# A routed mixture of experts: gating inside the expert block, and a scatter that adds rows in memory

## The reference, cut to what matters

```python
def hierarchical_moe(xn, w_rg, b_rg, w_re, b_re, w_g, w_u, w_d):
    ...                                  # a group and 2 of its 8 experts for each token: expert_idx, gates
    # 32 experts, blocks of 128 rows; each expert's rows are padded to whole blocks
    x_pad = jnp.zeros((n_blocks * MOE_BLOCK, d), xt.dtype).at[dest].set(xt[token_idx[order]])
    def expert_block(args):
        xb, e = args
        hb = jax.nn.silu(xb @ w_g[e]) * (xb @ w_u[e])
        return hb @ w_d[e]
    y = y_pad[dest] * gates[order][:, None].astype(y_pad.dtype)
    out = jnp.zeros((t, d), xt.dtype).at[token_idx[order]].add(y)
x = x + hierarchical_moe(rms_norm(x, norm_ffn[l]), ...)
return rms_norm(x, norm_final)
```

## Time and profile before

| What | Value |
|---|---|
| Time, median of 3 runs | 2952.2 us (2951.5 to 2953.98) |
| Span of the profiled execution, first to last instruction | 2942.6 us |
| That execution's own whole time | not listed; the median lies 9.6 us over its span |
| Busy share of the span: PE, DVE, ACT, POOL | 94%, 57%, 40%, 17% |
| Route stage | 2257.9 to about 2315.9 us |
| Expert blocks | 2315.9 to 2903.3 us |
| Last stage | 2903.4 to 2942.6 us |

### The profile page before, as it was taken

The page is one execution under the profiler, slowest core; times in us unless marked ns, Lnnn a source line. Parts: engine busy times, 40 slices in busy tenths (PEclk is TensorE's granted clock), DMA queues, the critical chain, the costliest instruction groups (busy, mean ns, idle before and its releaser), DMA issues. The chain is left out here.

```text
span 2942.6 us, 38553 instructions
## 1 busy us (share of the span) xinstructions
PE 2752.8 (94%) x14688; PEld 2400.7 (82%) x14688; DVE 1679.9 (57%) x2116; ACT 1179.4 (40%) x1703; POOL 513.8 (17%) x299
## 2 busy tenths in 40 slices
PE   8989999998899999999998999788998899999993
PEld 7989999898789999988776889566777588888883
DVE  5356654561434334333434732675534799999997
ACT  4342333421311111112334212664433377777774
POOL 3000000003122212200100000002610144444441
PEclk9999999999999999999998999899999899999997
DMA  5342223233211111112423111112302599999996
GB/s 193 106 131 94 94 84 131 100 118 129 81 48 50 43 49 50 43 50 93 150 71 105 40 50 58 58 51 87 112 26 113 180 410 421 413 413 417 412 415 250
DMA packets 244299, 436.94 MB, mean 148 GB/s; under 512 B 21698, under 2 KB 180690, under 8 KB 218594
## 3 DMA queue, kind: packets, MB, share of 16 engines
q1 hardware_dynamic: 234690, 400.88, 37.9%
q0 software_dynamic: 9504, 34.61, 2.9%
HBM read 375.54 MB, written 59.90 MB: 148 GB/s over the span
## 5 line engine op out<-in xcount | busy, mean ns | idle before, releaser
L3518 DVE TENSOR_TENSOR k_w_lo<-k_raw,k_w_hi 128x2048 fp32r<-128x2048 f32 x192 | 433.7, 2289 | 34.4 <-ACT k_w_hi L3454 30.1
L3454 ACT CAST k_w_hi<-k_raw 128x2048 fp32r<-128x2048 f32 x192 | 363.1, 1911 | 64.3 <-PE bank L3372 41.3
L120 PE MATMUL bank<-u_ffn_hi,f_w_hi 128*128 128x342 f32 (+1 forms) x840 | 292.1, 348 | 5.6 <-POOL f_w_lo L1333 5.6
L122 PE MATMUL bank<-u_ffn_hi,f_w_lo 128*128 128x342 f32 (+1 forms) x840 | 292.9, 349 | 0.0
L121 PE MATMUL bank<-u_ffn_lo,f_w_hi 128*128 128x342 f32 (+1 forms) x840 | 292.7, 348 | 0.0
L120 PE MATMUL bank<-u_hi,p_w_hi 128*128 128x342 f32 (+2 forms) x720 | 236.9, 329 | 9.0 <-DVEq L889 6.0
L121 PE MATMUL bank<-u_lo,p_w_hi 128*128 128x342 f32 (+2 forms) x720 | 231.1, 321 | 0.0
L122 PE MATMUL bank<-u_hi,p_w_lo 128*128 128x342 f32 (+2 forms) x720 | 230.8, 321 | 0.0
L3370 PE MATMUL bank<-k_w_hi,k_x_hi 128*128 128x512 f32 x512 | 203.0, 397 | 1.3 <-DVE k_x_lo L3524 1.0
L3372 PE MATMUL bank<-k_w_hi,k_x_lo 128*128 128x512 f32 x512 | 199.8, 390 | 0.0
L3371 PE MATMUL bank<-k_w_lo,k_x_hi 128*128 128x512 f32 x512 | 199.3, 389 | 0.0
(11 more groups left out here) (570 smaller groups left out, 6728.9 us busy)
## 6 DMA issues: line engine op xcount, KB each, us to landing
k_raw<-in_w_e_gate_dram SPq DMA_DIRECT2D x64, 1024.0 KB, 6.8
k_raw<-in_w_e_up_dram SPq DMA_DIRECT2D x64, 1024.0 KB, 7.3
k_raw<-in_w_e_down_dram SPq DMA_DIRECT2D x64, 1024.0 KB, 7.9
d_raw<-in_ffn_w_down_dram SPq DMA_DIRECT2D x44, 512.0 KB, 3.4
p_w<-in_w_in_dram SPq DMA_DIRECT2D x34, 512.0 KB, 4.3
f_raw<-in_ffn_w_gate_dram SPq DMA_DIRECT2D x22, 512.0 KB, 3.7
f_raw<-in_ffn_w_up_dram SPq DMA_DIRECT2D x22, 512.0 KB, 3.6
gate_scratch<-g_out SPq DMA_DIRECT2D x20, 513.0 KB, 6.3
```

Of the source, the lines that this page charges most:

```text
L120: pe.matmul(out, wh[:, t, :], xh[t][:, c:c + n], start=t == 0, stop=False)
L122: m = pe.matmul(out, wl[:, t, :], xh[t][:, c:c + n], start=False, stop=t == tiles - 1)
L3454: act.copy(wh[:, q, :], raw[:, r, :]).then_inc(hi_made, 1)
L3518: dve.tensor_tensor(wl[:, q, :], raw[:, r, :], wh[:, q, :], ALU.subtract).then_inc(lo_made, 1)
```

## The change

The two gates are no longer applied at the end. Each row of an expert block gets its gate (`weight`, one column of 128 rows for each block) as a factor in `gated`, on the hidden values. The list matmuls in the route stage therefore make two things, 96 columns in place of 48: the list of rows and the list of gates. SP stores `h` itself to memory (`sum_scratch`, 8 DMAs of 512 KiB) between the stores of the normalised rows. The scatter of an expert block adds its rows to those rows of `sum_scratch` (`compute_op=ALU.add`); both experts of a token add to the same row. Spare places add to rows behind row 1024. The last stage loads 8 times 512 KiB, norms and stores.

```diff
 stage_route:
+        gates = buffer(inner, nc, "r_gates", [P, 2 * NB])
-        in_block = buffer(inner, nc, "r_in_block", [P, 2 * NB, MAXB])
+        in_block = buffer(inner, nc, "r_in_block", [P, 2 * NB, 2, MAXB])
@@ SP
+            def rows_out(n):
+                sp.wait_ge(x_kept, n + 1)
+                if n in SHARED:
+                    sp.wait_ge(x_half, SHARED.index(n) + 1)
+                sp.dma_start(sum_d[n * P:(n + 1) * P, :].rearrange("p (k t) -> p k t", t=P), rows_of(h, n)).then_inc(h_stored, 16)
             for n in range(NB):
+                if n < NB - 2:
+                    rows_out(n)
+                if n == NB - 3:
+                    rows_out(NB - 2)
+                    rows_out(NB - 1)
                 sp.wait_ge(xn_made, n + 1)
                 sp.dma_start(xn_d[n * P:(n + 1) * P, :], xn[:, n % 4, :]).then_inc(stored[n % 4], 16)
             for s in range(4):
                 sp.wait_ge(stored[s], 16 * (NB // 4))
+            sp.wait_ge(h_stored, 16 * NB)
@@ PE
-                m = pe.matmul(bank[7][:, 0:MAXB], at_place[:, c, :], in_block[:, c, :], start=c == 0, stop=c == 2 * NB - 1)
+                m = pe.matmul(bank[7][:, 0:2 * MAXB], at_place[:, c, :], in_block[:, c, :, :], start=c == 0, stop=c == 2 * NB - 1)
@@ DVE, blocks_of(j), called twice
-                then(dve.tensor_tensor(in_block[:, half, :], *marks(begin[:, half], MAXB, begins[:, :]), ALU.is_equal))
-                return dve.tensor_tensor(in_block[:, half, :], in_block[:, half, :], own[:, half].unsqueeze(2).to_broadcast([P, NB, MAXB]), ALU.mult)
+                then(dve.tensor_tensor(in_block[:, half, 0, :], *marks(begin[:, half], MAXB, begins[:, :]), ALU.is_equal))
+                then(dve.tensor_tensor(in_block[:, half, 1, :], in_block[:, half, 0, :], gates[:, half].unsqueeze(2).to_broadcast([P, NB, MAXB]), ALU.mult))
+                return dve.tensor_tensor(in_block[:, half, 0, :], in_block[:, half, 0, :], own[:, half].unsqueeze(2).to_broadcast([P, NB, MAXB]), ALU.mult)
@@ DVE, the last instructions of the stage
             then(dve.tensor_scalar(token[:, :], assigned[:, :], SEQ - 1, None, ALU.bitwise_and))
+            then(dve.tensor_copy(weight[:, 0:MAXB], bank[7][:, MAXB:2 * MAXB]))
 stage_experts:
+        total = h[:, :, :].rearrange("p k t -> p (k t)").rearrange("p (b d) -> p b d", d=D)
@@ SP, last stage
             for b in range(NB):
-                if b >= RAW:
-                    sp.wait_ge(mixed, b - RAW + 1)
-                for j in range(2):
-                    sp.dma_start(raw[:, b % RAW, j * D:(j + 1) * D], y_d[j * SEQ + b * P:j * SEQ + (b + 1) * P, :]).then_inc(loaded[b % RAW], 16)
+                sp.dma_start(total[:, b, :], sum_d[b * P:(b + 1) * P, :]).then_inc(loaded[b], 16)
             for b in range(NB):
                 sp.wait_ge(normed, b + 1)
-                sp.dma_start(out[0, b * P:(b + 1) * P, :].rearrange("p (k t) -> p k t", t=P), rows_of(h, b)).then_inc(out_stored, 16)
+                sp.dma_start(out[0, b * P:(b + 1) * P, :], total[:, b, :]).then_inc(out_stored, 16)
@@ POOL, scatter
-                pool.indirect_dma_start(out=y_d, out_offset=bass.IndirectOffsetOnAxis(ap=to[:, s:s + 1], axis=0),
-                                        in_=y[:, s, :], in_offset=None).then_inc(stored[s], 16)
+                pool.indirect_dma_start(out=sum_d, out_offset=bass.IndirectOffsetOnAxis(ap=to[:, s:s + 1], axis=0),
+                                        in_=y[:, s, :], in_offset=None, compute_op=ALU.add).then_inc(stored[s], 16)
@@ ACT, last stage, for each b
-                act.wait_ge(mixed, b + 1)
-                act.activation(wide(sq[:, :]), rows_of(h, b), ACT.Square, accum_out=ss[:, 0, b:b + 1]).then_inc(squared, 1)
+                act.wait_ge(loaded[b], 16)
+                act.activation(sq[:, :], total[:, b, :], ACT.Square, accum_out=ss[:, 0, b:b + 1]).then_inc(squared, 1)
@@ DVE, gated
-                dve.tensor_tensor(hb[:, :].rearrange("p (k q) -> p q k", k=KE), sg[:, :].rearrange("p (q k) -> p q k", k=KE),
-                                  bank[3][:, :].rearrange("p (q k) -> p q k", k=KE), ALU.mult).then_inc(hb_made, 1)
+                dve.scalar_tensor_tensor(hb[:, :].rearrange("p (k q) -> p q k", k=KE), sg[:, :].rearrange("p (q k) -> p q k", k=KE), weight[:, ds(b, 1)],
+                                         bank[3][:, :].rearrange("p (q k) -> p q k", k=KE), ALU.mult, ALU.mult).then_inc(hb_made, 1)
@@ DVE, last stage
-                dve.scalar_tensor_tensor(rows_of(h, b), made(0, b), gates[:, b:b + 1], rows_of(h, b), ALU.mult, ALU.add).then_inc(first, 1)
-                dve.wait_ge(first, b + 1)
-                dve.scalar_tensor_tensor(rows_of(h, b), made(1, b), gates[:, NB + b:NB + b + 1], rows_of(h, b), ALU.mult, ALU.add).then_inc(mixed, 1)
-                if b:
-                    norm(b - 1)
-            norm(NB - 1)
+            for b in range(NB):
+                dve.wait_ge(rooted, b + 1)
+                ...
+                dve.scalar_tensor_tensor(total[:, b, :], total[:, b, :], ss[:, 2, b:b + 1], gain[:, :], ALU.mult, ALU.mult).then_inc(normed, 1)
```

More of the change, by code:

```diff
@@ L2942, in rows_of, with stage_route @@
     return h[:, :, b * P:(b + 1) * P]
-def stage_route(nc, ctx, A, K, bank, h, gates, assigned, token, table, xn_d, wr, br, gain, raw, pieces_in):
-    (turned, x_kept, x_half, lmm, squared, roots, xn_made, stored_a, stored_b, stored_c, stored_d, rmm, cnt, iotas, rows, act_rows, marked, weighed, listed, lt_kept, l_turned) = sems(
-        ctx, nc, "r", "turned x_kept x_half lmm squared roots xn_made stored_a stored_b stored_c stored_d rmm cnt iotas rows act_rows marked weighed listed lt_kept l_turned")
+def stage_route(nc, ctx, A, K, bank, h, weight, assigned, token, table, xn_d, sum_d, wr, br, gain, raw, pieces_in):
+    (turned, x_kept, x_half, lmm, squared, roots, xn_made, stored_a, stored_b, stored_c, stored_d, rmm, cnt, iotas, rows, act_rows, marked, weighed, listed, lt_kept, l_turned, h_stored) = sems(
+        ctx, nc, "r", "turned x_kept x_half lmm squared roots xn_made stored_a stored_b stored_c stored_d rmm cnt iotas rows act_rows marked weighed listed lt_kept l_turned h_stored")
     ident, ones, eps, lower = (K[n] for n in ("ident", "ones", "eps", "lower"))
@@ L3003, in _ @@
             pool.iota(begins[:, :], [[P, MAXB]], base=0, channel_multiplier=0, allow_small_or_imprecise_dtypes=True).then_inc(iotas, 1)
-            pool.iota(own[:, :], [[P, 2 * NB]], base=-2 * SEQ, channel_multiplier=1, allow_small_or_imprecise_dtypes=True).then_inc(iotas, 1)
-            pool.iota(spare[:, :], [[1, 1]], base=2 * SEQ, channel_multiplier=1, allow_small_or_imprecise_dtypes=True).then_inc(iotas, 1)
+            pool.iota(own[:, :].rearrange("p (j b) -> p j b", j=2), [[0, 2], [P, NB]], base=-SEQ, channel_multiplier=1, allow_small_or_imprecise_dtypes=True).then_inc(iotas, 1)
+            pool.iota(spare[:, :], [[1, 1]], base=SEQ, channel_multiplier=1, allow_small_or_imprecise_dtypes=True).then_inc(iotas, 1)
         @block.tensor
@@ L3226, in _, with stage_experts @@
             then(dve.tensor_scalar(token[:, :], assigned[:, :], SEQ - 1, None, ALU.bitwise_and))
-def stage_experts(nc, ctx, A, K, bank, assigned, token, table, xn_d, y_d, raw, pieces_in, h, gates, out):
+            then(dve.tensor_copy(weight[:, 0:MAXB], bank[7][:, MAXB:2 * MAXB]))
+def stage_experts(nc, ctx, A, K, bank, assigned, token, table, xn_d, sum_d, raw, pieces_in, h, weight, out):
     (g0, g1, turned, x_hi, x_lo, used, hi_made, lo_made, silu_made, hb_made, hturned, h_hi, h_lo,
@@ L3235, in stage_experts @@
     gathered, stored = (g0, g1), (s0, s1)
-    all_stored, gain_in, first, mixed, squared, normed, out_stored = sems(ctx, nc, "o2", "all_stored gain_in first mixed squared normed out_stored")
-    loaded = sems(ctx, nc, "o2", " ".join(f"in{r}" for r in range(RAW)))
+    all_stored, gain_in, squared, logs, rooted, normed, out_stored = sems(ctx, nc, "o2", "all_stored gain_in squared logs rooted normed out_stored")
+    loaded = sems(ctx, nc, "o2", " ".join(f"in{b}" for b in range(NB)))
     ident, eps = K["ident"], K["eps"]
@@ L3502, in _ @@
             for b in range(NB):
-                act.wait_ge(mixed, b + 1)
+                act.wait_ge(loaded[b], 16)
                 if b:
-                    act.wait_ge(squared, 3 * b)
-                act.activation(wide(sq[:, :]), rows_of(h, b), ACT.Square, accum_out=ss[:, 0, b:b + 1]).then_inc(squared, 1)
[L3507 to L3510, removed]
+                    act.wait_ge(squared, b)
+                act.activation(sq[:, :], total[:, b, :], ACT.Square, accum_out=ss[:, 0, b:b + 1]).then_inc(squared, 1)
+                act.wait_ge(squared, b + 1)
+                act.activation(ss[:, 1, b:b + 1], ss[:, 0, b:b + 1], ACT.Ln, bias=eps[:, 0:1], scale=1.0 / D).then_inc(logs, 1)
+                act.wait_ge(logs, b + 1)
+                act.activation(ss[:, 2, b:b + 1], ss[:, 1, b:b + 1], ACT.Exp, scale=-0.5).then_inc(rooted, 1)
```

(7 more changed lines are left out.)

9 lines of the change are left out of this document (removed).

## The result

The changed kernel takes 2967.4 us (median of 4 runs, 2966.5 to 2968.6), the kernel before in the same session 2953.1 (2951.5 to 2954.3): ratio 1.005, 95% interval 1.0038 to 1.0062. It is slower by 14.3 us; the forecast was 2968.

A forecast was written before the change was run, and what follows sets the result against it. PE set the pace, with DMA 0.27 us a turn from full and becoming the bound. Route +4.3, expert blocks +26, last scatter +1.3, last stage -16.1: +15.5 us, span 2958.1, median 2968 us; range 2937 to 3006.

The forecast's parts named there:

- Price of an adding row: Expert blocks' scatter: adding reads memory too, 1.05 MB in place of 0.52, so +1.27 us a scatter at 414 GB/s.
- rival E: Expert blocks: DVE bounds the turn through `gated`, each 0.1 us beyond 0.9 us costing 3; E or other, chance 0.02.
- PE busy below 96: Sign in the expert windows: PE busy below 96 of 100 us, idle time ended by DVE's low parts and ACT's casts.
- expert term: Expert blocks: 29 adding scatters at 1.27 us, 36.8, less 11.5 of reserve; taken as +26 us.
- reserve: Expert blocks: 11.5 us absorbed, from 5.5 us by which weights land ahead of use and 6 of unused DMA time.
- Last scatter: End of the expert blocks: the last scatter's landing, 3.3 us after issue, is on the path and grows by 1.3 us.
- Last stage: Halved loads, 16 of DVE's 24 operations gone: 38.7 us become 22.6, DMA's floor; gain 16.1, bounds 14 to 17.5.
- Route: Route stage: +4.3 us together, 2.8 for storing `h` and 1.45 for two gate products and the copy of `weight`.
- A: Expert blocks' scatter: the added read is free, so the kernel gets faster, sum -11.8, 2940.5 us; chance 0.24.
- D: Expert blocks' scatter: a price in between, about 0.6 to 0.95 us, gives 2947 to 2957, no change; chance 0.07.
- C: Expert blocks' scatter: adding costs more than a second read; at 2.54 us the total is 3005, open above; chance 0.18.
- decision point of 0.78: Added price in us a scatter up to which the free-read rival decides, where 29p - 11.5 + p equals 11.8.

The follow-up runs named there:

- e7: Changed kernel with each block's rows scattered twice, plainly, to sum_scratch and a second scratch, in place of one adding scatter; sums left out: 2967.0 us.
- e1: Changed kernel with the adding taken out of the scatter, so rows overwrite each other and sums are left out: 2940.1 us.
- e8: Changed kernel with only every other block's scatter adding, the others overwriting, so half of the sums are left out: 2945.8 us.
- e10: Changed kernel with padding rows skipped in the scatter and real rows dealt by p // 4 and by the half, to meet 16 engines: 2946.1 us.
- e3: Changed kernel with a bound on the adding scatter that skips the padding rows behind row 1023; result unchanged: 2970.0 us.
- e4: Changed kernel with the stores of h placed behind the first two stores of normalised rows: 2963.6 us.
- e5: Changed kernel with the edits of e3 and e4 together, padding rows skipped and h stored later: 2964.6 us.
- e6: Changed kernel with padding rows skipped and ranks spread over the block, rank 16b+a at row 8a+b: 2962.0 us.
- e9: Changed kernel with the edits of e6 and e4 together, rows spread and skipped and h stored later: 2962.2 us.
- e11: Changed kernel with the edits of e10 and e4 together, rows dealt over 16 engines and h stored later: 2942.7 us, ratio 0.9968.

## Why the prediction came out right

**Price of an adding row: right.** 1.27 us was taken from twice the traffic, and 1.30 was measured. e7 shows that it is occupancy of the engines like that of a second plain scatter. The rule of "Collectives: The Full Stack" (section "The bandwidth ceiling: the fold count and why AG ≠ RS ≠ AR") in the Trainium skill, two source reads and so half of the rate, agrees with this case in the price: 328 ns in place of 159 for the same row. The two reads themselves are not shown.

**Who bounds: right.** DMA, not POOL and not DVE, through ACT's casts; turn 18.56 against 18.7 forecast; landing 11.4 in 11 to 12. `gated` (rival E) costs nothing, by e1. Wrong was "PE busy below 96": it is 96.75 to 99.3, and the count of matmuls, down by 2 to 5%, would have been the row to name. The idle time did end by a low part of DVE's, but by that of the gathered rows, not of the weights.

**Size of the expert term: near, by two errors that offset.** It was 29 x 1.27 less a reserve of 11.5. Measured: 29 x 1.30 = 37.7, and the stage grew by 23.4. First error, the reserve. It rested on the step "The highest rate of a 100 us window of this mixture is 421 GB/s", hence 17.43 us and 0.27 unused a turn. That window wasn't DMA's ceiling: e8 and the changed kernel give 17.33 and 17.28, so 0.4 was unused; with the latter, 29 x 0.43 + 5.5 of lead is 18 us. Second error, a stall that was not in the sum. POOL's timeline and PE's wait, early in the stage:

```profile
2388.13 7.15 POOL L3326 DMA_INDIRECT k_rows<-xn_scratch,k_from  x1 [0.82 <-POOLq L3324]
```

```profile
PE bank L3371 <- DMA k_rows<-xn_scratch,k_from: 2.0, 1, 2.0
```

The gather right behind the stage's first scatter costs POOL 7.15 us here (0.99 in before and in e1), its rows come late, and PE waits once. PE's clock then drops, in windows of 2 us around it:

```profile
2402.00:2404.00 2.00, 0.70 (x4) 0.71 (x5) 1.91 (x2) 0.00 (x0) 1.21 (x3) 0.86 1.02 428
2404.00:2406.00 2.00, 2.00 (x9) 1.81 (x8) 0.15 (x1) 0.77 (x2) 0.72 (x1) 0.50 1.04 393
2406.00:2408.00 2.00, 2.00 (x9) 1.59 (x8) 1.14 (x2) 2.00 (x2) 0.00 (x0) 0.79 1.04 305
```

Of these 6 us, 0.28 + 1.0 + 0.42 = 1.7 us of work are lost to the lower clock, on top of 2.0 of waiting: 3.7 us. 37.7 - 18 + 3.7 = 23.4. That the three terms meet the measurement so exactly is partly luck: the reserve is good to one or two us, and its 0.43 comes from the measured turn itself. A count that needs neither price nor reserve agrees: 23 turns, the seventh to the 29th, are 0.87 us over PE's 17.70, 20.0 us in all, and 3.7 for the stall. The slow gather and PE's wait show in every kernel that adds. e7 has the wait too, but there the gather takes 1.00 us and it is POOL's copy of the index column ahead of it that takes 6.67 (0.20 in e1). In e10, whose expert blocks are 3.7 us over before with PE otherwise full, it is all that is left; where the clock stayed up, it cost less (1.9 us in e8's first two turns). Why POOL takes so long there wasn't tested.

**Last scatter: the term was too small.** Forecast +1.3, measured +2.8: its landing went from 3.3 to 6.06 us, POOL's own part of it from 0.98 to 1.57. The step "Its landing, 3.3 us after issue, is on the path: +1.3" priced it by throughput. Alone on its engines the scatter has 8 rows an engine, 8 x 0.169 = 1.35, and 0.6 are POOL's; the other 0.8 I can't place. Rows are the smaller part: in e10 the last scatter has 45 real rows dealt over 16 engines, and still lands after 5.19 us.

**Last stage: right, 0.8 us too fast.** 22.6 forecast, 23.4 measured (from the first load's issue, 2942.99, to 2966.37). The floor taken, 16 transfers in one queue, holds; the dip between loads and stores, 1.0 us, was left out.

**Route: right.** +4.3 against +4.2: 2.4 for `h` ahead in the queue (2.8 forecast) and 1.4 for the two products and the copy (1.45), on the pair with equal PE clock (before and e3, +3.9 together); the other 0.3 of the +4.2 came with PE's slow start. The sign that the prediction named, a wait near 4 us before the second pair of normalised blocks, was 3.3 us in e3 and only 1.2 in the changed kernel, where that slow start hid the rest. The list matmuls stayed covered. Late `h` stores cost nothing more, as assumed, though SP's issues took up to 4.89 us while the transfers were queued.

**Rivals.** A is excluded by e1 and e7: the added read isn't free. D would need a price under 0.95, and C one of 2.5; it is 1.30. The sign did hang on that one price: half of the adding (e8, 0.65 a turn) would have made the kernel faster, as the decision point of 0.78 said.

## What to carry to other kernels

Before moving an addition from a vector engine into a DMA, look at the DMA share where the DMA will run, not where the addition was: here it saved 15 us in a stage that runs once and cost 23 in one whose DMA engines had some 2% to spare. Price an adding row as two plain ones. If part of the rows is padding, skip it, but look at how the real rows fall on the 16 engines: a mean share hides that half of them do all of the work. A share near 1 doesn't tell how much is left either: it was 1.01 in the kernel before, with PE as the bound, and 1.02 after. Dealing the real rows evenly was worth 24 us here (e3 to e10).

## What the runs showed that was not expected

- A 4 KiB row of an indirect scatter that adds holds its engine for 327 to 328 ns, a plain one for 159.
- With half of the rows skipped, bytes fell and time didn't (e3, turn 18.64 at 378 GB/s); the same bytes on all engines gave 17.71 (e10, 398 GB/s).
- POOL's time for one indirect DMA grows with what it does: 0.98 us plain and 1.57 adding where it runs unhindered, 6.7 to 7.3 for the stage's first scatter, and 7.15 for the gather behind it where that scatter adds.
- After much the same wait of 1.5 to 2.7 us PE's granted clock fell to 0.50 in four profiled runs (the changed kernel, e3, e7, e10), and stayed at 1.00 in the six others that have the wait (e4, e5, e6, e8, e9, e11).
